# Inputs of the attention and output stages loaded one stage earlier, and head 1's sums of the unit loop moved behind the next masks

## The reference, cut to what matters

```
c  = centred_conv(proj[:, :o0])            # 3 taps over tokens
# RWKV7, both directions, 8 heads of 64:
for t: sa = state @ a_t
       state = state * w_t + outer(sa, b_t) + outer(v_t, k_t)
       y_t = state @ r_t
y  = norm(y) * ln_g + ln_b + bonus         # bonus = sum(r*k*r_k) * v
# differential attention, 4 heads, two maps m of width 64 each:
lam = exp(sum(lv[0]*lv[1])) - exp(sum(lv[2]*lv[3])) + lam_init
s   = q @ k.T - slope * |qpos - kpos|
att = softmax(s[m=0]) - lam * softmax(s[m=1])
o   = rmsnorm(att @ v, subln)
# output:
h   = x + concat(y * silu(g0), o * silu(g1)) @ w_out
e   = rmsnorm(p @ ple_proj, ple_norm)
out = h + sigmoid(h @ gate_w + gate_b) * e
```

## Time and profile before

| | |
|---|---|
| median of 3 runs | 3745.22 us (3741.4 to 3746.01) |
| profiled execution, its own time | 3744.75 us |
| its span in the profile | 3743.0 us |
| TensorE busy | 3479.2 us, 93% |
| TensorE weight loads, beside it | 2281.9 us |
| VectorE busy | 2335.3 us, 62% |
| ScalarE busy | 1409.3 us, 38% |
| GpSimd busy | 382.0 us, 10% |
| mean granted TensorE clock | 0.975 of full speed |
| HBM read, written | 194.95 MB, 157.29 MB |
| DMA over the span | mean 95 GB/s |

### The profile page before, as it was taken

How to read it: one execution, slowest core, us unless ns; L and a number is a source line. 1 busy time by engine, 2 the same in 40 slices (tenths; PEclk the granted TensorE clock), 3 DMA queues, 4 the chain that set the end, 5 groups by cost and what they waited for, 6 DMA issues and landing times. The chain is left out here.

```text
span 3743.0 us, 56377 instructions
## 1 busy us (share of the span) xinstructions
PE 3479.2 (93%) x21081; PEld 2281.9 (61%) x21081; DVE 2335.3 (62%) x4283; ACT 1409.3 (38%) x2572; POOL 382.0 (10%) x679
## 2 busy tenths in 40 slices
PE   7999998799999997999999986899999959999998
PEld 5788886344444446777777773566777634444444
DVE  3555555799999944566665655777777734444443
ACT  3445444132332322222222204566666622323322
POOL 0343333000000002222222200000000000000000
PEclk9999999899999998999999998999999979999999
DMA  4353435522222224433333352300000041222121
GB/s 145 134 163 116 138 120 174 184 73 102 100 101 92 84 87 131 132 116 106 107 107 107 107 164 79 96 11 14 11 14 11 12 185 54 80 80 80 59 74 44
DMA packets 307944, 355.04 MB, mean 95 GB/s; under 512 B 122380, under 2 KB 234712, under 8 KB 305312
## 3 DMA queue, kind: packets, MB, share of 16 engines
q1 hardware_dynamic: 294304, 341.82, 27.8%
q10 hardware_dynamic: 13440, 10.49, 0.9%
HBM read 194.95 MB, written 157.29 MB: 94 GB/s over the span
## 5 line engine op out<-in xcount | busy, mean ns | idle before, releaser
L595 PE MATMUL cv_pj<-cv_uT,w 128*128 128x257 f32 (+1 forms) x2240 | 503.3, 382 | 0.0
L595 PEld LDWEIGHTS cv_pj<-cv_uT,w 128*128 128x128 f32 (+1 forms) x2240 | 410.4, 186 | 89.1 <-issue 21.8
L1592 PE MATMUL at_g<-at_kT,at_qz 64*128 64x512 f32 x1088 | 303.6, 634 | 30.8 <-DMA at_kT<-scratch_q_kT 25.5
L875 DVE TENSOR_TENSOR rs_tt<-rs_tt,rs_tmp 128x63 f32<-128x63 f32 (+31 forms) x315 | 288.9, 917 | 10.8
L873 DVE TENSOR_TENSOR rs_tmp<-rs_tt,rs_al 128x63 f32<-128x63 f32 (+31 forms) x315 | 284.2, 902 | 15.6 <-DMA rs_al<-scratch_ablk 6.0
L1615 PEld LDWEIGHTS at_pb<-at_v,at_attT 128*128 128x128 f32 x2176 | 249.8, 192 | 64.6 <-issue 47.0
L1544 DVE CUSTOM_DVE_ANT_0 at_sca<-at_g,at_nd 128x1024 f32<-128x1024 f32 (+1 forms) x144 | 167.8, 1166 | 183.5 <-PE at_g L1592 183.0
L1863 PE MATMUL fn_gb<-fn_wg,fn_hT 128*128 128x512 f32 x640 | 278.0, 592 | 1.7 <-ACT fn_hT L1722 1.7
L1863 PE MATMUL fn_hb<-fn_wo,fn_mixT 128*128 128x512 f32 x640 | 279.4, 594 | 0.3 <-ACT fn_mixT L1722 0.3
L1615 PE MATMUL at_pb<-at_v,at_attT 128*128 128x128 f32 x2176 | 265.1, 279 | 13.0 <-ACT at_attT L1502 13.0
L944 PE MATMUL rs_tm<-w,x_pair 128*128 128x512 f32 x480 | 214.1, 604 | 32.4 <-DMA rs_gains<-in_da_k_norm_dram 19.8
(11 more groups left out here) (256 smaller groups left out, 5773.7 us busy)
## 6 DMA issues: line engine op xcount, KB each, us to landing
un_pk<-scratch_packs SPq DMA_DIRECT2D x80, 640.0 KB, 3.9
scratch_packs<-cv_pk SPq DMA_DIRECT2D x19, 2048.0 KB, 6.7
w<-in_w_in_dram SPq DMA_DIRECT2D x6, 2048.0 KB, 12.0
x_pair<-in_x_dram SPq DMA_DIRECT2D x20, 512.0 KB, 3.6
scratch_uT<-cv_uT SPq DMA_DIRECT2D x5, 2048.0 KB, 7.9
scratch_ablk<-cv_ab SPq DMA_DIRECT2D x80, 128.0 KB, 3.6
rs_al<-scratch_ablk SPq DMA_DIRECT2D x5, 2048.0 KB, 8.9
scratch_gate<-rs_tok_out SPq DMA_DIRECT2D x40, 256.0 KB, 2.4
```

Of the source, the lines that this page charges most:

```text
L595: last = nc.tensor.matmul(pj[n % 3][0:r, 0:HALF], w[:, c, m * P:m * P + r], uT[b % 2][:, c, HALF * hf:HALF * hf + HALF], start=(c == 0), s ...
L875: last = nc.vector.tensor_tensor(target, target, part, ALU.add)
L1592: last = nc.tensor.matmul(gb[m][:, c * 512:(c + 1) * 512], qz[par][rows, h, :], kT[rows, h, at:at + 512], start=True, stop=True)
```

## The change

What it does, phase by phase:

- **Convolution, rest.** The last corner block goes to a free part of another buffer (`ab_last`), so its copy doesn't wait for a store. TensorE's wait for all constants in the rest phase moves from the front to behind the products of the second tile.
- **Unit.** (The loop is written out in the program: 80 bodies.) VectorE masks `scores(n+2, 0)` at the end of body n, behind the sums of head 0, instead of `scores(n+1, 0)` at the front of body n. The sums of head 1 of unit n move into body n+1, between the second masks and the wait for the store. ScalarE's carry copy of head 1 moves with them, into body n+1 between `turned` and the wz copy. SyncE, GpSimd and TensorE keep their code, but store, loads and `ad` wait for signals that now come later.
- **Ahead loads.** The classes `Ahead` and `OutputAhead` own buffers and semaphores that outlive a phase. The chain phase loads the identity (once for all later phases) and attention 0's inputs behind its own loads, and works out attention 0's distances at its front. Attention 0 does the same for attention 1, one part of the loads per tile and the distances in eight pieces over its last two tiles. Attention 1 loads, at its front, what the first mixing of the output phase needs. Each phase waits for these loads before its end.
- **Attention.** The lambda work moves behind VectorE's second reduction. With 4 tiles the loop is unrolled. The keys' and constants' waits at TensorE's front are gone or already met.
- **Output.** `wo` comes in two halves with tile 1's inputs between them, x and p of tile 0 behind; `y_in` of tile 1 stands between the two halves of tile 0's product, and its mixing ahead of tile 0's `residual`.

The diff, cut to its core:

```diff
@@ conv_phase: SyncE store, ScalarE corner
+        ab_last = win[NK % 2][:, 0:2, 0:512].rearrange("p d (h q t) -> p d h q t", h=2, q=NQ)
-                if k:
+                if k and k < NK - 1:
                     act.wait_ge(s["ab_stored"], 64 * k)
...
@@ rest_phase: TensorE
-            pe.wait_ge(s["const"], 96)
             for t in range(NT):
...
+                if t == 1:
+                    pe.wait_ge(s["const"], 96)
                 if t:
                     turn(t - 1)
@@ unit_phase: ScalarE
                 if more:
                     turned(*nxt(n, j, par))
+                if n:
+                    own(n - 1, 1 - par, 1)
                 act.wait_ge(s["wz_ready"], n + 1)
...
-                    act.wait_ge(s["carry_evac"], n * 4 + 2 * h + 10)
-                    nc.scalar.copy(carry_at(n, par, hs, slice(0, 2), 192, 256), ...
+                    if h == 0:
+                        own(n, par, 0)
+                if not more:
+                    own(n, par, 1)
+            def own(n, par, h):          # the two lines taken out above
@@ unit_phase: VectorE
-                if more:
-                    masked(m, pm, 0)
                 dve.wait_ge(s["q_ready"], n + 1)
...
                 if more:
                     masked(m, pm, 1)
+                if n:
+                    sums(n - 1, 1 - par, 1)
+                if more:
                     dve.wait_ge(s[f"local{pm}"], jm * 16 + 16)
                     products(m, pm)
...
+                sums(n, par, 0)
+                if n + 2 < NI:
+                    masked(n + 2, par, 0)
+                if not more:
+                    sums(n, par, 1)
...
             products(0, 0)
+            masked(1, 1, 0)
             chunks(dve, body)
@@ chain_phase: SyncE behind its own loads; GpSimd; VectorE's front
+            sp.dma_start(ident[:, :], ident_d).then_inc(s["ident"], 16)
+            for part in range(4):
+                following.load(sp, part)
+            sp.wait_ge(s["ident"], 16)
+            following.landed(sp)
+            following.places()                   # GpSimd
+            for part in range(8):
+                following.distances(dve, part)   # VectorE
+class Ahead:
...
+    def load(self, sp, part):
+        if part == 0:
+            sp.dma_start(self.q0[:, :, :], self.q_v[0]).then_inc(self.s["q0"], 16)
+        for h in ((0, 1), (2, 3), (), ())[part]:
+            sp.dma_start(self.kT[:, h, :], self.k_v[:, h, :]).then_inc(self.s[f"k{h}"], 16)
+        for h in ((), (0,), (1, 2), (3,))[part]:
+            sp.dma_start(self.v[:, :, h * P:(h + 1) * P], self.v_v[:, :, h * P:(h + 1) * P]).then_inc(self.s[f"v{h}"], 16)
...
+    def places(self):
+        self.nc.gpsimd.iota(self.wide[:, :], ...).then_inc(self.s["wide0"], 1)
+    def distances(self, dve, part):
+        width = (2 * self.S - P) // 8
+        columns = self.wide[:, part * width:(part + 1) * width]
+        dve.wait_ge(self.s["wide0"], 1)
+        self.nc.vector.scalar_tensor_tensor(columns, columns, -1.0, columns, ALU.mult, ALU.min).then_inc(self.s["wide1"], 1)
+class OutputAhead:               # y, o, bonus, two gates of tile 0; three rows
...
@@ attention_phase
-            if count > 2:
+            if count == 4:
+                body(0, 0, 0, True)
+                body(1, 0, 1, True)
+            elif count > 2:
...
             load_q(1, 1)
+            if output:
+                output.load(sp)
...
                     load_q(n + 2, par)
+                if following:
+                    following.load(sp, n)
...
             reduce(0, 0, 0, 0, False)
             reduce(0, 0, 0, 1, False)
+            dve.wait_ge(s["const"], 16)
+            ...                              # the lambda operations, from the front
...
+                    if following and n >= count - 2:
+                        following.distances(dve, (n - count + 2) * HD + h)
-            pe.wait_ge(s["const"], 32)       # TensorE
@@ output_phase: SyncE, VectorE, TensorE
+            sp.dma_start(wo[:, :, 0:HALF], w_v[0][:, :, 0:HALF]).then_inc(s["wo0"], 16)
+            load(1, 1)
+            sp.dma_start(wo[:, :, HALF:D_MODEL], w_v[0][:, :, HALF:D_MODEL]).then_inc(s["wo1"], 16)
+            for dst, src in ((x[0][:, :], x_t[0]), (p[0][:, :], p_t[0])):
+                sp.dma_start(dst, src).then_inc(s["in0"], 16)
             sp.dma_start(wp[:, :, :], w_v[2]).then_inc(s["wp"], 16)
...
+            mixing(1, 0, 1, 3)
+            dve.wait_ge(s["in0"], 112)
             residual(0, 0)
-            mixing(1, 0, 1, 4)
...
-            product(hb, mixT, wo, KC, "h_mm")
-            y_in(0, 1, 4, 0)
+            for i in range(2):
+                pe.wait_ge(s[f"wo{i}"], 16)
+                ...                          # half i of the product
+                if i == 0:
+                    y_in(0, 1, 3, 1)
```

More of the change, by code:

```diff
@@ L1376, in attention_phase @@
+def attention_phase(nc, name, first, count, q_kT, o_tok, lam_d, ident, here, following, output):
     S = count * P
@@ L1383, in attention_phase @@
     with Phase(nc, name) as ph:
[L1384 to L1388, removed]
+        kT, v, wide = here.kT, here.v, here.wide
+        qz = [here.q0, ph.sb("qz1", [P, HD, P])]
         nd = [ph.sb(f"nd{i}", [P, S]) for i in range(2)]
@@ L1464, in _ @@
                 sp.wait_ge(s[f"stored{par}"], count * 8 + 16)
+            if output:
+                output.landed(sp)
+            if following:
+                following.landed(sp)
         @block.gpsimd
         def _(pool):
-            nc.gpsimd.iota(wide[:, :], pattern=[[-1, 2 * S - P]], base=S - P, channel_multiplier=1,
-                           allow_small_or_imprecise_dtypes=True).then_inc(s["wide0"], 1)
+            if following:
+                following.places()
         @block.scalar
@@ L1774, in wide, with mixing @@
                 return v.unsqueeze(2).broadcast_to([P, heads, 512 // heads])
-            def mixing(n, j, par, q):
+            def mixing(n, j, par, q, loads=7):
                 st = Steps(dve, s["step"], n * PER)
@@ L1949, in hybrid_encoder @@
             unit_phase(nc, tokens, packs, tblk, nblk, carry, local, kept, a["ident"], full)
[L1950 to L1952 removed]
+            chain_phase(nc, tokens, sequences, carry, local, kept, y, ahead, ident, a["ident"])
+        rows = [a[n] for n in ("rw_ln_g", "rw_ln_b", "da_subln", "ple_norm", "ple_gate_b")]
+        output = OutputAhead(nc, ctx, y, o_tok, local, gates, rows)
+        with ExitStack() as late:
+            for i, (first, count) in enumerate(sequences):
+                here, ahead = ahead, Ahead(nc, late, f"at{i + 1}", *sequences[i + 1], q_kT, v_tok) if i + 1 < len(sequences) else None
+                attention_phase(nc, f"at{i}", first, count, q_kT, o_tok, a["da_lambda"], ident, here, ahead, None if ahead else output)
         output_phase(nc, tokens, a["x"].rearrange("(c p) d -> c p d", p=P), a["p"].rearrange("(c p) d -> c p d", p=P), y, local, gates,
                      o_tok, out.rearrange("(c p) d -> c p d", p=P), a["w_out"][0], a["ple_proj"][0], a["ple_gate_w"][0],
[L1955 removed]
+                     rows, ident, output)
 def kernel(**inputs):
```

176 lines of the change are left out of this document (95 added, 81 removed).

## The result

| | before | after |
|---|---|---|
| median | 3745.22 us (5 runs, 3741.3 to 3748.4) | 3725.52 us (5 runs, 3718.5 to 3727.1) |
| ratio, 95% interval | 1 | 0.9943 [0.9933, 0.9954] |
| span of the profiled run | 3743.0 us | 3723.8 us |

What follows compares the result with a forecast made beforehand. TensorE, busy 93% of the span, was taken as the bound, so only its idle time could be won. Gains of 0.3 + 16.6 + 0.9 + 1.2 + 7.9 + 21.0 = 47.9 us gave 3697 us, range 3681 to 3714.

Steps and rivals of the forecast that it cites:

- The store's landing: Unit loop: VectorE's new wait for the store makes a loop of 8.4 us, under the body's 9.2, costing nothing.
- L: Unit loop: time from the store's issue to its landing, taken as 1.7 us; the loop through it is 6.74 + L.
- rival C: Unit loop: L is 3.4, the store loop 10.14, each body 0.73 us longer than before; total 3772; chance 0.06.
- At most 2.6: Unit loop: stores landed in 1.7 us, at most 2.6, given as evidence against a binding store loop.
- The wz copy: Unit loop: ScalarE's carry copy delays the wz copy, so each body gains 0.21 us, 16.6 over 79 bodies.
- Rival A: Unit loop gains nothing, as the wz copy behind the carry copy replaces the wait for masks; 3714; chance 0.15.
- Rest and convolution: Convolution's end gains 0.3 us; the rest stage gains 0, since VectorE bounds it to 1313.
- Chain and attention 0: Chain stage and attention 0: TensorE starts 2.8 us earlier, less 0.8 for lambda work and 0.8 for distances: net 1.2.
- Rival D: Early loads don't help: they hold back chain stage's and attention 0's ends by what they save; 3717; chance 0.05.
- Attention 1: Attention 1: TensorE starts 9.2 us earlier, less 1.3 for the lambda work: net 7.9 us (5 to 10).
- Output stage: Output stage: the second hb product starts 41.0 us into the stage instead of 62.0, so 21.0 us won.
- rival B: Stage borders: TensorE's clock holds there; its size is not in the text; chance 0.17.

Runs made afterwards that it cites:

- three_local: The changed kernel with a third local_out buffer, so VectorE's products wait for the store of unit n-2 instead of n-1: 3701.7 us, ratio 0.9882.
- Own_free: The changed kernel with ScalarE's carry copy of head 1 made at once in body n, not in body n+1: 3709.0 us, ratio 0.9909.
- early: three_local with attention 0's keys, values and queries loaded in unit bodies 30, 40, 50 and 60, not at the chain phase's end: 3699.6 us, ratio 0.9881.
- shift26: The changed kernel with 26 more semaphore increments on TensorE, once, at the unit phase's front: 3729.2 us, ratio 0.9960.
- pad51: three_local with 51 more semaphore increments on TensorE in each unit body, ahead of the output products' waits: 4362.5 us, run once.
- both: The changed kernel with a third local_out buffer and head 1's carry copy made at once: 3680.0 us, ratio 0.9827.

## Why the prediction was wrong, step by step

- **The store's landing, the step that failed.** The prediction took L = 1.7 from the earlier trace rows for all bodies, found 8.4 under 9.2, and put the loop down at nothing; the other value, 3.4, went into rival C as a switch for all bodies at once, with a chance of 0.06. The formula held but for 0.14: the late bodies from body 25 on take 6.60 + L, each to 0.02 us (9.8 to 10.6, with L from 3.2 to 4.0). What was wrong was to treat L as one number. It is 1.7 in four bodies and 3 to 4 in the fifth, and three_local shows the price: 19.9 of the 25.9 us that are missing in the unit stage (21.4 over the 79 bodies; the clock in the last body hides the rest). "At most 2.6" was true of stores issued where they were, clear of the 16 KB fetches; the same edit moved them. The page of before lists 133 instruction packets of 16 KB and 67 smaller ones, and in its trace the stores that took 2.3 to 2.6 are those with a smaller one on them.
- **The wz copy.** The mechanism and each start up to 5.51 held to 0.01 us. The copy followed at the upper bound, 0.28, so 0.14 per body was won and not 0.21: 5.5 of the other 6.0 us. Rival A overstated it. Own_free puts its price at 0.29 per body. The start of head 1's sums at 4.72, 0.03 behind the masks' end, was an estimate of mine, and no row of before shows it. In the kernel after the masks end at 2059.94 and the sums start at 2059.96, 0.02 behind; they don't overlap, as line 1154 in the earlier trace rows does with the end of line 1157 (0.07).
- **Rest and convolution.** -0.4 and -0.1: right. TensorE started the rest stage 4.9 us earlier, and the stage was as long as before, since VectorE bounds it.
- **Chain and attention 0.** Forecast -1.2, measured +2.1. The last load landed 69.6 us into the stage, where 67.9 was forecast, and the stage ended 1.5 later. The forecast added up the time of ScalarE's y stores and of SyncE's new loads on the same engines, which no row of before shows. The runs do: in the kernel after both queues move data from 2262 to 2266, at 65.4% and 43.4% of the 16 engines, and with the loads taken away (early) the stage is 4.9 shorter. First to last output of attention 0 took 55.8 instead of 54.0. The distances cost about what was forecast (0.8): three heads take 3.70 instead of 3.53, and in three_local, which has them too, the whole is 54.7. The rest is the clock: the last two heads took 4.2 and 3.9 us instead of 3.3, because TensorE's granted clock fell within them (1.00 from 2332 to 2334, 0.54 from 2334 to 2336, then 0.50). The last head's product with the values waits the same 0.73 us for ScalarE in both kernels, but takes 2.08 us instead of 1.16 (before, then after):

```profile
2328.71 1.16 PE L1615 MATMUL at_pb<-at_v,at_attT 128*128 128x128 f32 x8 [0.73 <-ACT at_attT L1502]
...
2337.78 2.08 PE L1698 MATMUL at_pb<-at_v,at_attT 128*128 128x128 f32 x8 [0.73 <-ACT at_attT L1588]
```

  In three_local that stretch is at full clock (1.00 from 2312 to 2318), and the product takes 1.16. Rival D had the direction and was too strong for the other stages.
- **Attention 1.** -7.3 against -7.9: right.
- **Output stage.** -21.9 against -21.0: right in sum, by luck in part. The second mixing starts 25.0 us into the stage, where 23.8 was forecast, and from it to the second product hb it takes 14.6 us and not 17.17, because the clock holds there (1.00 from 3052 to 3063): the second hb starts at 39.6 (41.0 forecast). Nothing waited for weights. The product e ahead of the second hb, before (clock 0.69) and after (1.00):

```profile
3081.64 5.19 PE L1863 MATMUL fn_eb<-fn_wp,fn_pT 128*128 128x512 f32 x8
...
3063.68 3.60 PE L1944 MATMUL fn_eb<-fn_wp,fn_pT 128*128 128x512 f32 x8
```

- **The clock.** At the chain stage's end the granted clock of the kernel after falls to 0.50 while TensorE stands still, as it did before (0.60 from 2255 to 2257, then 0.50). In windows of 2 us (window, length; us of PE, PEld, DVE, ACT and POOL; PEclk; DMA share; GB/s):

```profile
2262.00:2264.00 2.00, 0.00 (x0) 0.00 (x0) 0.00 (x0) 0.00 (x0) 0.00 (x0) 0.62 1.10 380
2264.00:2266.00 2.00, 0.00 (x0) 0.00 (x0) 0.00 (x0) 0.00 (x0) 0.00 (x0) 0.50 1.08 384
```

Attention 1's first scores again took 3.79 us, as in the earlier trace rows, though TensorE idled only 4.15 before them and not 13.02:

```profile
2344.01 3.79 PE L1675 MATMUL at_g<-at_kT,at_qz 64*128 64x512 f32 x8 [4.15 <-DVEq L1602]
```

In attention 1, then, rival B, a clock that holds at the borders, did not come true: the clock had fallen at 2334, in attention 0's last heads, and was still at 0.50. But at the second mixing and in the last unit body it did, in this trace. At the second mixing TensorE idled 3.03 us and not 10.11 and kept the full clock (1.00, where before it was 0.54 from 3070.5 to 3078), 2.6 us. In the last unit body it kept it, too: the output products to the end of the body take 2.9 us, where they took 5.3 (before, then after):

```profile
2182.00:2184.00 2.00, 2.00 (x21) 1.88 (x20) 0.00 (x0) 0.00 (x0) 0.00 (x0) 0.50 0.00 0
...
2192.00:2194.00 2.00, 2.00 (x22) 1.86 (x16) 0.22 (x1) 0.24 (x1) 0.00 (x0) 1.00 0.00 0
```

So the clock gave about 5 us that the forecast didn't count, and took 1.4 at attention 0's end. In the rows from 2262 the DMA share is over 1: the engines are full to 2266, the chain stage's price.

With the store loop free the kernel takes 3702, and with the wz copy off the path too 3680: the order of the edit was sound, and two resources that it newly leaned on were not.

## What to carry to other kernels

When an edit puts an engine behind the landing of a DMA, write down the loop as "fixed part + L" and then ask for the late landings, not the median: how often, and what else comes onto the DMA engines in the half microsecond in which those packets go (here from 0.84 to 1.38 us behind the issue). Here instruction fetches were among it (94 that started 0.6 to 1.24 behind an issue, 94 late stores), and in shift26 their place in the body did not follow from their place in the program. One more buffer took the whole question away (three_local: bodies of 9.26 or 9.27); the kilobyte per partition for it lay unused in a buffer of a later phase. Compare stage lengths first: here they put 26 of 29 missing microseconds in one place. And before a stretch's gain or loss is put down to an edit, compare the granted clock of that stretch in both kernels.

## What the hardware showed beyond the forecast

- One 16 KB instruction packet takes 0.9 to 1.8 us in the unit loop of the kernel after. Where one started 0.99 to 1.15 us behind the issue of a 128 KB store (12 of the bodies from 20 on), the store landed at 3.2 to 4.0 us instead of 1.7, its last eight packets of 128 behind the fetch.
- An increment of a semaphore on TensorE ahead of its matmuls is dear here: in a body of pad51 (at 2017) the 51 more let its matmuls stand still for 6.9 us, about 0.13 us each; I had expected 0.025, an estimate that no run had shown. The bodies grew from 9.27 us to 17.1 and more, and the granted clock falls there, too: it is 0.70 to 0.80 over a body, and 1.00 in three_local, and the products of a body take 11.0 us (2017 to 2034.1) instead of 8.9.
- A carry copy of 0.26 us ahead of the wz copy cost 0.29 per body on the path (bodies of 9.27 in three_local, 8.98 in both): the wz copy starts 0.28 behind the carry copy's start, with its input ready.
